# Two-block transformer kernel on one core: layers written out, attention of the first block by pairs of heads

## The chip, the cores and the metric

The kernel runs on one core of one Trainium2 chip. The metric is the device time of one execution in microseconds, as the median of several runs. The profile is of one further execution. Its engines are PE (TensorE), DVE (VectorE), ACT (ScalarE), POOL (GpSimd) and SP (SyncE, which here only issues DMAs).

## The reference, cut to what matters

256 tokens of width 1024 pass through a first block of two hybrid layers and then a second block. All arithmetic is in float32.

```
DEPTH = 2                      # layers of the first block, each with its own weights
def hybrid_layer(x, mem, ...):
    z = rms_norm(x, g_mix) @ w_in                       # 1024 x 5632
    o_a = dilated_mixer(rope(q)*s, rope(k), v)          # 2 output heads, 3 dilations each, one softmax over all
    o_b = moba_attn(rope(q)*s, rope(k), v)              # 6 heads; with 256 tokens plain causal attention
    o_m = memory_attn(q_m*s, rms_norm(mem), w_mkv)      # 4 heads over 256 memory rows
    y = gates[0]*(o_a @ w_pa) + gates[1]*(o_b @ w_pb) + gates[2]*(o_m @ w_pm)
    x = x + y @ w_o                                     # gates = sigmoid of 3 x 1024 columns of z
    return x + square(relu(rms_norm(x) @ w_up)) @ w_down   # 1024 -> 4096 -> 1024
```

The second block (`*_2` inputs) has modulation from a condition vector, latent attention with 8 heads, an mLSTM branch and 16 experts. The weights of an expert are three matrices of 1024 x 1024 (4 MB each), so 192 MB of the 393 MB that the kernel reads belong to the experts.

## The kernel before

Every layer of the first block streams its weights in 64 **units** of 1 MB (4 row chunks of 128 by 512 columns, `layer_units`). They pass through `R1 = 4` ring slots: SP issues the load of unit u when PE is done with unit u-4 (`load`, semaphore `slots_free`). Most units are **split**: ACT copies the unit in a rounded form to `ring_hi` (`split_hi`, L535), then DVE or POOL writes the rest, unit minus high part, over the unit itself, `ring_lo` (`split_lo`, L554), and PE makes three products low by high, high by low and high by high for each pair of tiles (`split_product`, L1683 to L1685). `LO_VECTOR` says which units DVE splits (4, 6, 8 and the even ones from 34), POOL does the others. The activations are held feature-major and split in the same way in `hT_hi` and `hT_lo`. Units 10 and 11 (memory keys and values) and 24 to 27 (branch projections) are plain float32 products (L1675).

A layer, in the order of PE's program: transposes of x (`half_to_features`, L1722) and units 0 to 11; rope on DVE and the transposes of q and k; **attention** with the gate units 12 to 23 in between; the branch projections, units 24 to 27, of which DVE makes y (L2051, L2060); units 28 to 31 (`w_out`), 32 to 47 (`w_up`) with the squares transposed behind each tile (`squares`, L1872), 48 to 63 (`w_down`) with small products for the modulation (L1899). The two layers are one loop body, `Fori(0, DEPTH)`, on each engine.

Attention runs in `NJ` jobs, each one head and one tile of 128 queries: 4 dilated, 12 causal, 8 memory, so 24, in 25 rounds of a pipeline. In round j, PE computes the scores of job j (L1788), transposes the weights of job j-1 (L1798), does half of a gate part (6 split products), multiplies the transposed weights of job j-1 with the values (L1821), and does the other half. DVE masks the scores and takes the maximum (L2028), ACT takes exp in SBUF with the sum (L2173), DVE divides (L2008, L2010), ACT copies the transposed weights (L2168) and the output (L2179) out of PSUM, splits a unit (L535) in every second round, and applies tanh to a finished gate (L2188).

The order on each engine is written by hand; there is no scheduler, and engines run in order. A head has 64 features, so scores use 64 of PE's 128 rows and outputs 64 of its 128 columns:

```
last = pe.matmul(flat[j % 2][:, col:col + wide * P], qkT[rows, qc, q],
                 keys[rows, kc, kt * P:(kt + wide) * P], start=True, stop=True)   # rows = 64 partitions
```

The experts run in four groups of four. PE computes the four experts of a group at once in the four 32-column strips of the array (L939), from a ring of `RE = R + 4 = 12` slots of 1 MB that SP fills in order (L612). At the end the result is scattered to tokens (L956), added to x (L1364), normalised (L1910 to L1920, L2120, L2122), multiplied with a row (L1386) and stored by one DMA (L617).

## Time and profile before

| | us |
|---|---|
| median of 3 runs (1917.25 to 1918.72) | 1918.7 |
| the profiled execution | 1913.6 |
| its span | 1911.7 |
| PE busy | 1600.2 (84%) |
| DVE busy | 606.2 (32%) |
| ACT busy | 501.0 (26%) |
| POOL busy | 487.8 (26%) |

PE is busy nine tenths or more in most slices of the first 1440 us, and seven tenths behind that, where the DMA engines are busy throughout at 421 GB/s. The busy shares say where to look; what a stretch costs is read from its length and from what its work would need without pauses.

### The profile page before, as it was taken

How to read it: one execution, taken by the hardware profiler on the slowest of the kernel's cores; microseconds unless marked ns; L12 is line 12 of the kernel's file. 1: busy time of each engine (PE TensorE's matmuls, PEld its weight loads, DVE VectorE, ACT ScalarE, POOL GpSimd, SP SyncE). 2: the span in 40 equal slices, each digit the busy share in tenths (PEclk: the TensorE clock that was granted, in tenths of full speed). 3: DMA queues.
4: the chain of work that ended last, by engine and by line, in shares of the span. 5: the costliest groups of instructions: out<-in, count | busy, mean ns of one | idle time of the engine just before them, and what ended most of it. 6: DMA issues, size and time to landing. Idle time of an engine off the chain costs nothing. (4 is left out here: it accounts for less than half of the span.)

```text
span 1911.7 us, 18589 instructions
## 1 busy us (share of the span) xinstructions
PE 1600.2 (84%) x7308; PEld 1027.1 (54%) x7308; DVE 606.2 (32%) x900; ACT 501.0 (26%) x675; POOL 487.8 (26%) x147
## 2 busy tenths in 40 slices
PE   5999989899999998989959999969768567675764
PEld 4765568777766557877657865547343113131111
DVE  4334345421524443542253126753240000000001
ACT  4254234323435433333233313423010000000000
POOL 5434162324534424433455521000000000000000
PEclk9999999999999999999979999989869889899888
DMA  6523335577543334549723462000229999999994
GB/s 217 179 92 111 110 133 176 176 285 276 166 155 98 112 124 133 176 150 351 250 66 111 133 225 93 0 13 1 77 110 399 421 422 421 421 422 421 421 422 207
DMA packets 125044, 395.49 MB, mean 207 GB/s; under 512 B 6799, under 2 KB 10692, under 8 KB 100380
## 3 DMA queue, kind: packets, MB, share of 16 engines
q1 hardware_dynamic: 123308, 389.70, 54.9%
q0 software_dynamic: 1648, 4.56, 0.7%
q8 instruction: 61, 1.00, 0.2%
q14 instruction: 27, 0.22, 0.0%
HBM read 393.18 MB, written 1.05 MB: 206 GB/s over the span
## 5 line engine op out<-in xcount | busy, mean ns | idle before, releaser
L554 POOL TENSOR_TENSOR ring_lo<-ring,ring_hi 128x2048 fp32r<-128x2048 f32 x80 | 370.0, 4629 | 546.0 <-ACT ring_hi L535 545.9
L1683 PE MATMUL psum<-ring_hi,hT_lo 128*128 128x512 f32 (+2 forms) x880 | 360.0, 409 | 36.2 <-DVE hT_lo L1927 11.7
L1685 PE MATMUL psum<-ring_hi,hT_hi 128*128 128x512 f32 (+2 forms) x880 | 347.2, 395 | 0.0
L1684 PE MATMUL psum<-ring_lo,hT_hi 128*128 128x512 f32 (+2 forms) x880 | 346.2, 393 | 0.0
L535 ACT ACTIVATE ring_hi<-ring 128x2048 fp32r<-128x2048 f32 x116 | 222.0, 1914 | 378.4 <-DMA ring<-in_w_down 138.7
L939 PE MATMUL psum<-ring,arena 128*32 128x512 f32 x1024 | 200.2, 678 | 89.4 <-DMA ring<-in_w_e_up 33.2
L1683 PEld LDWEIGHTS psum<-ring_hi,hT_lo 128*128 128x128 f32 x880 | 169.2, 192 | 80.1 <-issue 21.2
L1685 PEld LDWEIGHTS psum<-ring_hi,hT_hi 128*128 128x128 f32 x880 | 168.3, 191 | 36.6
L1684 PEld LDWEIGHTS psum<-ring_lo,hT_hi 128*128 128x128 f32 x880 | 169.0, 192 | 31.6 <-issue 0.5
L939 PEld LDWEIGHTS psum<-ring,arena 128*32 128x32 f32 x1024 | 44.0, 121 | 242.2 <-issue 83.6
L554 DVE TENSOR_TENSOR ring_lo<-ring,ring_hi 128x2048 fp32r<-128x2048 f32 x36 | 86.4, 2400 | 249.7 <-ACT ring_hi L535 249.7
L939 PE MATMUL psum<-arena 128*32 128x512 f32 x512 | 80.6, 787 | 54.3 <-DMA arena<-in_w_e_down 31.1
L1675 PE MATMUL psum<-ring,arena 128*128 128x512 f32 (+1 forms) x272 | 113.0, 574 | 0.9 <-ACT arena L2179 0.9
L547 POOL TENSOR_TENSOR ring_lo<-ring,ring_hi 128x2048 fp32r<-128x2048 f32 (+2 forms) x20 | 87.4, 4375 | 69.2 <-ACT ring_hi L542 69.2
L1683 PE MATMUL psum<-ring_hi,uT_lo 128*128 128x512 f32 x256 | 102.9, 402 | 0.0
L1684 PE MATMUL psum<-ring_lo,uT_hi 128*128 128x512 f32 x256 | 102.3, 400 | 0.0
L1685 PE MATMUL psum<-ring_hi,uT_hi 128*128 128x512 f32 x256 | 100.8, 394 | 0.0
L1675 PEld LDWEIGHTS psum<-ring,arena 128*128 128x128 f32 x272 | 51.3, 190 | 58.2 <-issue 50.6
L939 PEld LDWEIGHTS psum<-arena 128*32 128x32 f32 x512 | 19.6, 138 | 108.6 <-issue 61.3
L1545 ACT ACTIVATE arena<-psum 128x512 f32<-128x512 f32 x8 | 4.3, 595 | 248.1 <-PE psum L939 248.1
L2010 DVE TENSOR_SCALAR arena<-arena,rden 128x256 f32<-128x256 f32 (+3 forms) x48 | 60.8, 1267 | 1.7
L1683 PEld LDWEIGHTS psum<-ring_hi,uT_lo 128*128 128x128 f32 x256 | 49.2, 192 | 16.2 <-issue 5.0
(323 smaller groups left out, 1664.5 us busy)
## 6 DMA issues: line engine op xcount, KB each, us to landing
ring<-in_w_in SPq DMA_DIRECT2D x60, 1024.0 KB, 5.2
ring<-in_w_e_gate SPq DMA_DIRECT2D x48, 1024.0 KB, 20.1
ring<-in_w_e_up SPq DMA_DIRECT2D x48, 1024.0 KB, 21.6
ring<-in_w_up SPq DMA_DIRECT2D x32, 1024.0 KB, 5.2
ring<-in_w_down SPq DMA_DIRECT2D x32, 1024.0 KB, 6.1
arena<-in_w_e_down SPq DMA_DIRECT2D x32, 1024.0 KB, 19.9
ring<-in_w_e_down SPq DMA_DIRECT2D x32, 1024.0 KB, 22.3
arena<-in_w_e_gate SPq DMA_DIRECT2D x16, 1024.0 KB, 18.0
```

What stands on the lines that cost most here:

```text
L535: act.activation(slot_hi(u), slot(u), ACT.Copy).then_inc(hi_sb, 1)
L547: pool.tensor_tensor(slot_lo(u)[:, :, 0:n], slot(u)[:, :, 0:n], slot_hi(u)[:, :, 0:n].bitcast(F32), ALU.subtract)\
L554: eng.tensor_tensor(slot_lo(u), slot(u), slot_hi(u).bitcast(F32), ALU.subtract).then_inc(done, 1)
L939: mm = pe.matmul(psum[32 * j:32 * j + 32, bank + n, :], lhsT[:, 2 * q + c, 32 * j:32 * j + 32], both[:, c * D + n * UN:c * D + (n + 1) * U ...
L1545: act.activation(hid[:, n, :], psum[:, n, :], ACT.Silu).then_inc(hid_a, 1)
L1675: last = pe.matmul(dst, lhsT(k0 + k), slot(u)[:, first + k, 0:n], start=start and k == 0, stop=stop and k == nk - 1)
L1683: pe.matmul(dst, lo(k0 + k), w_hi, start=start and k == 0, stop=False)
L1684: pe.matmul(dst, hi(k0 + k), w_lo, start=False, stop=False)
L1685: last = pe.matmul(dst, hi(k0 + k), w_hi, start=False, stop=stop and k == nk - 1)
L2010: dve.tensor_scalar(S[:, i % 3, 0:wide], S[:, i % 3, 0:wide], rden[:, i:i + 1], None, ALU.mult)\
```

## The change

1. The two layers are written out (`for l in range(DEPTH)` in place of `Fori`); waits compare with constants, and the copies of per-layer data (`g_now`, `silu_now`) go. POOL splits all units except unit 0 of layer 0 and the even units from 50, which stay on DVE.
2. Attention: 13 jobs in 14 rounds. A job holds two heads of a pair, one in each half of the partitions, except the two dilated ones of the second query tile, which hold one head. PE alternates between the two heads in scores and outputs; the two heads' scores lie in different PSUM banks. ACT writes exp into PSUM over the scores, and DVE multiplies from there into SBUF for both heads in one instruction. DVE now does maximum, scale, reciprocal and multiply of job j before it turns to job j+1. The gate work is cut in 48 parts of 6 products, spread over 27 places by `gate_parts`. ACT splits one unit at the end of each of the rounds 0 to 8.
3. Branch projections: three pairs of PSUM banks in turn instead of two, and y is summed from PSUM.
4. The last squares (`squares(7)`) are transposed behind unit 48; the first half of x for the next layer is transposed in the middle of unit 63, the second half behind unit 0 of the next layer.
5. `w_out`/`w_up`: ACT makes the first half of `hT_hi` before it splits unit 34.
6. Start: x and the small rows are loaded from ACT's queue, the memory rows and large constants only when x has landed; DVE splits unit 0.
7. Experts: `RE = R + 8`, 16 slots. The last expert pass finishes one half of the columns first; the last normalisation goes tile by tile, with the table of the square root loaded ahead, and two stores.

```diff
-LO_VECTOR = [4, 6, 8] + list(range(34, UNITS1, 2))
-LO_POOL = [u for u in SPLIT if u not in LO_VECTOR]
+LO_VECTOR = [(l, u) for l in range(DEPTH) for u in SPLIT if (l == 0 and u == 0) or (u >= 50 and u % 2 == 0)]
+LO_POOL = [(l, u) for l in range(DEPTH) for u in SPLIT if (l, u) not in LO_VECTOR]
...
+    job("dilated", 0, 0, [(HD * h, dilated(h, 0)) for h in range(2)])
     for h in range(2):
+        job("dilated", 1, 0, [(HD * h, dilated(h, 1))])
+    for pair in range(3):
         for t in range(TT):
...
+            job("causal", t, 1 + pair, [(HD * i, [(6 + pair, 9 + pair, kt, ("z", 3 * WA + 2 * WB + HD * (2 * pair + i)))
+                                                  for kt in range(t + 1)]) for i in range(2)])
...
+def gate_parts(j, place):
+
+    at = lambda slot: (2 * GATE_PARTS * slot + 2 * NJ + 1) // (2 * (2 * NJ + 1))
+    slot = 2 * j + place if j < NJ else 2 * NJ
...
-RE = R + 4
+RE = R + 8
...
                         while i < len(bl):
...
+                            for h, (base, blocks) in enumerate(job["heads"]):
+                                qc, kc, kt, _ = blocks[i]
+                                rows = slice(base, base + HD)
+                                last = pe.matmul(to[:, h, i * P:(i + wide) * P], qkT[rows, qc, q],
+                                                 keys[rows, kc, kt * P:(kt + wide) * P], start=True, stop=True)
...
+                        for i in range(n):
+                            for h, (base, blocks) in enumerate(job["heads"]):
...
+                                last = pe.matmul(flat[2][base:base + HD, 768:768 + P], v, PT[:, (j - 1) % 2, h * n + i, :],
+                                                 start=i == 0, stop=i == n - 1)
...
-                        dve.tensor_scalar(S[:, i % 3, 0:wide], S[:, i % 3, 0:wide], rden[:, i:i + 1], None, ALU.mult)\
+                    dve.tensor_tensor(weights_of(j), scores(j), rden[:, c0:c0 + nh].unsqueeze(2).to_broadcast([P, nh, wide]), ALU.mult)\
...
-                    if j % 2 and 15 + j // 2 < 24:
-                        split_hi(act, l, 15 + j // 2)
...
+                    if 15 + j < 24:
+                        split_hi(act, l, 15 + j)
...
-                        part.append(z[:, :, c0:c0 + UN])
-                        dve.scalar_tensor_tensor(out=part[b], in0=part[b], scalar=1.0, in1=DB[i % 2][:, :, :],
-                                                 op0=ALU.add, op1=ALU.mult).then_inc(pj_sb, 1)
+                        part = y if b == 0 else DB[PJ[i]][:, :, :]
+                        ins = dve.scalar_tensor_tensor(out=part, in0=z[:, :, c0:c0 + UN], scalar=1.0, in1=DB[PJ[i]][:, :, :],
+                                                       op0=ALU.add, op1=ALU.mult)
...
-                squares(7)
                 for kg in range(8):
...
+                            if t == 1 and u == UNITS1 - 1 and l + 1 < DEPTH:
+                                pe.wait_ge(dn_x, 2 * l + 1)
+                                half_to_features(x, 0)
...
+                        if u == 48:
+                            squares(7)
...
-                high_parts(32, 34)
-                high_half(0, g_now[:, 2, :], l * 8 + 7)
+                high_parts(32, 33)
+                high_half(0, g_feat[:, 2, l, :], l * 8 + 7)
+                high_parts(34, 34)
```

The order that results, at three places. PE's program in the causal part of attention; L1683 to L1685 are gate products, L1788 the scores of a job, L1798 the transposes and L1821 the outputs of the job before. Before:

```order
L1821 MATMUL psum<-arena 64x128 x2
L1683 MATMUL psum<-ring_hi,hT_lo 128x512
L1684 MATMUL psum<-ring_lo,hT_hi 128x512
L1685 MATMUL psum<-ring_hi,hT_hi 128x512
L1683 MATMUL psum<-ring_hi,hT_lo 128x512
L1684 MATMUL psum<-ring_lo,hT_hi 128x512
L1685 MATMUL psum<-ring_hi,hT_hi 128x512
L1779 REGISTER_ALU
L1788 MATMUL psum<-arena 128x256
L1794 REGISTER_ALU
L1798 MATMUL psum<-consts,arena 128x128
```

The same place of the changed kernel, where L1872 are the outputs, L1848 the scores, L1727 to L1729 the gate products and L1860 the transposes; this is the first causal job behind the dilated ones:

```order
L1872 MATMUL psum<-arena 64x128 x6
L1848 MATMUL psum<-arena 128x128 x2
L1727 MATMUL psum<-ring_hi,hT_lo 128x512
L1728 MATMUL psum<-ring_lo,hT_hi 128x512
L1729 MATMUL psum<-ring_hi,hT_hi 128x512
L1727 MATMUL psum<-ring_hi,hT_lo 128x512
L1728 MATMUL psum<-ring_lo,hT_hi 128x512
L1729 MATMUL psum<-ring_hi,hT_hi 128x512
L1860 MATMUL psum<-consts,arena 128x128 x6
```

Outputs and scores now stand next to each other, both heads' matmuls in one row, and the gate products moved between scores and transposes and between transposes and outputs.

ACT in the same part of attention. Before, L2168 copies transposed weights, L2173 is exp, L2179 copies an output, L535 splits a unit:

```order
L2168 ACTIVATE arena<-psum 128x128
L2172 REGISTER_ALU
L2173 ACTIVATE arena,den<-arena,nmx 128x256
L2179 ACTIVATE arena<-psum 64x128
L535 ACTIVATE ring_hi<-ring 128x2048
L2165 REGISTER_ALU
L2168 ACTIVATE arena<-psum 128x256
L2172 REGISTER_ALU
L2173 ACTIVATE arena,den<-arena,nmx 128x128
L2179 ACTIVATE arena<-psum 64x128
```

And of the changed kernel, with exp in L2242, tanh of a gate in L2234, the copy of weights in L2251, of an output in L2257 and the split in L561:

```order
L2242 ACTIVATE psum,den<-arena,nmx 128x256 x2
L2234 ACTIVATE arena<-psum,rms 128x512
L2251 ACTIVATE arena<-psum 128x256
L2234 ACTIVATE arena<-psum,rms 128x512
L2257 ACTIVATE arena<-psum 128x128
L561 ACTIVATE ring_hi<-ring 128x2048
L2242 ACTIVATE psum,den<-arena,nmx 128x128 x2
L2251 ACTIVATE arena<-psum 128x512
```

Exp of the next job moved ahead of the copy of the weights, and the split of a unit stands at the end of every round up to round 8, where before it stood in every second.

PE at the end of `w_up`. Before, the transposes of the last two squares (L1872) follow each other ahead of the first product of `w_down` (the one with uT):

```order
L1685 MATMUL psum<-ring_hi,hT_hi 128x512
L1867 REGISTER_ALU
L1869 REGISTER_ALU
L1872 MATMUL psum<-consts,arena 128x128 x8
L1867 REGISTER_ALU
L1869 REGISTER_ALU
L1872 MATMUL psum<-consts,arena 128x128 x8
L1683 MATMUL psum<-ring_hi,uT_lo 128x512
```

In the changed kernel the one transpose group (L1919) is followed by `w_down` at once:

```order
L1728 MATMUL psum<-ring_lo,hT_hi 128x512
L1729 MATMUL psum<-ring_hi,hT_hi 128x512
L1919 MATMUL psum<-consts,arena 128x128 x8
L1727 MATMUL psum<-ring_hi,uT_lo 128x512
L1728 MATMUL psum<-ring_lo,uT_hi 128x512
L1729 MATMUL psum<-ring_hi,uT_hi 128x512
```

The other group of eight moved behind the 24 products of unit 48.

## Rows read from the trace of the kernel before

**Rows 1.** Busy time of each engine by stretch (us), PE clock, DMA share, GB/s

```profile
24.60:102.50 77.90, 77.05 (x320) 58.16 (x320) 37.18 (x44) 26.76 (x26) 39.92 (x10) 1.00 0.49 160
102.50:223.30 120.80, 112.98 (x509) 75.43 (x509) 48.71 (x120) 54.70 (x118) 42.42 (x10) 1.00 0.30 97
223.30:304.50 81.20, 72.88 (x279) 51.42 (x280) 33.99 (x30) 27.10 (x29) 37.29 (x8) 0.96 0.44 144
304.50:376.30 71.80, 71.80 (x338) 59.13 (x337) 35.80 (x30) 28.58 (x19) 27.94 (x7) 1.00 0.54 176
376.30:384.20 7.90, 1.90 (x11) 1.67 (x10) 5.97 (x5) 2.17 (x2) 0.00 (x0) 0.82 0.40 133
...
485.50:491.20 5.70, 2.02 (x18) 1.75 (x17) 2.88 (x5) 2.68 (x9) 1.07 (x1) 1.00 0.57 190
...
566.70:687.50 120.80, 112.96 (x509) 75.46 (x509) 48.71 (x120) 54.71 (x118) 41.85 (x10) 1.00 0.30 97
...
1430.00:1887.50 457.50, 309.79 (x1657) 93.53 (x1658) 20.26 (x29) 14.00 (x25) 0.00 (x0) 0.89 0.99 413
```

**Rows 2.** PE's groups by shape in attention, 102.5 to 223.2 us

```profile
L1683 PE MATMUL psum<-ring_hi,hT_lo 128*128 128x512 f32 x96 | 42.3, 440 | 4.7 <-ACT arena L2188 4.7
...
L1821 PE MATMUL psum<-arena 128*64 128x128 f32 x104 | 16.5, 284 | 1.4 <-ACT arena L2168 1.4
L1788 PE MATMUL psum<-arena 64*128 64x256 f32 x40 | 12.9, 418 | 0.0
L1798 PE MATMUL psum<-consts,arena 128*128 128x128 f32 x52 | 10.9, 297 | 1.2 <-DVE arena L2010 1.2
L1788 PE MATMUL psum<-arena 64*128 64x128 f32 x24 | 4.8, 306 | 0.9 <-ACT arena L2160 0.9
```

**Rows 3.** Pieces of the chain that ended last: start, us, what

```profile
1857.86 3.73 PE psum L939 x32
...
1895.50 3.71 PE psum L956 x8
```

**Rows 4.** Timelines of DVE and POOL in attention and in the branch projections

```profile
133.09 0.35 DVE L2010 TENSOR_SCALAR arena<-arena,rden 128x256 f32<-128x256 f32 x1
...
136.85 3.38 DVE L2010 TENSOR_SCALAR arena<-arena,rden 128x128 f32<-128x128 f32 x1
...
249.18 4.63 DVE L2060 TENSOR_TENSOR xn<-xn,arena 128x1024 f32<-128x1024 f32 x1
...
135.58 4.57 POOL L554 TENSOR_TENSOR ring_lo<-ring,ring_hi 128x2048 fp32r<-128x2048 f32 x1 [6.23 <-ACT ring_hi L535]
...
248.15 14.67 POOL L554 TENSOR_TENSOR ring_lo<-ring,ring_hi 128x2048 fp32r<-128x2048 f32 x3 [1.31 <-ACT ring_hi L535]
```

**Rows 5.** Who waited for whom: 223.3 to 305 us, then 376 to 385 us

```profile
PE psum L1683 <- DVE hT_lo L1927: 4.9, 1, 4.9
...
PE psum L1722 <- DVE xn L2060: 3.4, 1, 3.4
...
PE psum L1872 <- DVE arena L2098: 6.0, 1, 6.0
```

**Rows 6.** PE's timeline at the start, SP's at the experts, DVE's and ACT's at the end

```profile
24.61 0.80 PE L1683 MATMUL psum<-ring_hi,hT_lo 128*128 128x512 f32 x1 [6.47 <-POOL ring_lo L554]
...
1434.94 2.07 SPq L612 DMA_DIRECT2D ring<-in_w_e_gate  x4
...
1901.66 1.28 ACT L2122 ACT_TABLE_LOAD   x1
...
1903.40 1.42 DVE L1920 TENSOR_SCALAR xn<-x,stat 128x1024 f32<-128x1024 f32 x2
...
1904.92 2.36 DVE L1386 TENSOR_TENSOR xn<-xn,arena 128x1024 f32<-128x1024 f32 x2
```

**Rows 7.** DMA issue with its landing time, and ACT's group of unit splits

```profile
ring<-in_w_in SPq DMA_DIRECT2D x60, 1024.0 KB, 5.2
...
L535 ACT ACTIVATE ring_hi<-ring 128x2048 fp32r<-128x2048 f32 x116 | 222.0, 1914 | 378.4 <-DMA ring<-in_w_down 138.7 <-DMA ring<-in_w_up 109.2 <-DMA ring<-in_w_in 71.8
```

More of the change, by code:

```diff
@@ L123 @@
 NJ = len(JOBS)
+NH = sum(len(job["heads"]) for job in JOBS)
+GATE_PARTS = 8 * 6
+def gate_parts(j, place):
+    at = lambda slot: (2 * GATE_PARTS * slot + 2 * NJ + 1) // (2 * (2 * NJ + 1))
+    slot = 2 * j + place if j < NJ else 2 * NJ
+    if j == NJ and place == 0:
+        return range(0)
+    return range(at(slot), at(slot + 1))
 def z_column(chunk):
@@ L272, in build @@
         turn_lo = sem("turn_lo")
-        gains = sem("gains")
         mem_g = sem("mem_g")
@@ L406, in build @@
         row_in = sem("row_in")
-        quad_in = sem("quad_in")
-        ctx_in = sem("ctx_in")
+        quad_in = [sem(f"quad_in{i}") for i in range((RE - R) // 4)]
         x_row = sem("x_row")
@@ L931, in experts @@
                 for q in rounds:
-                    for c in range(2):
-                        for n in range(2):
+                    ends = g == NE // EG - 1 and part == 2 and q == 3
+                    for c, n in ((0, 0), (1, 0), (0, 1), (1, 1)) if ends else ((0, 0), (0, 1), (1, 0), (1, 1)):
                             for j in range(EG):
@@ L943, in experts @@
                                     mm.then_inc(slots_free, 1)
+                            if ends and c == 1 and n == 0:
+                                mm.then_inc(y_half, 1)
             def gather(g):
@@ L1774, in _, with gate_part @@
                 pe.wait_ge(km_sb, l + 1)
+                def gate_part(p):
+                    g, kh, t, half = p // 8, p // 4 % 2, p // 2 % 2, p % 2
+                    u = 12 + p // 4
+                    if p % 4 == 0:
+                        unit_ready(u, l)
+                    if g and kh == 0 and half == 0:
+                        pe.wait_ge(g_tanh, l * 12 + 2 * (g - 1) + t + 1)
+                    last = split_product(DB[3][:, t, :], tokens(hT_hi, t), tokens(hT_lo, t), UC * kh + 2 * half, u, nk=2,
+                                         first=2 * half, start=kh == 0 and half == 0, stop=kh == 1 and half == 1)
+                    if kh == 1 and half == 1 and t == 0:
+                        last.then_inc(g_full, 1)
+                    if half == 1 and t == 1:
+                        last.then_inc(slots_free, 1)
@@ L1784, in _ @@
+                        i, bl = 0, job["heads"][0][1]
                         while i < len(bl):
-                            qc, kc, kt, _ = bl[i]
-                            wide = 2 if i + 1 < len(bl) and bl[i + 1][1] == kc else 1
-                            keys = kmT if job["kind"] == "memory" else qkT
-                            last = pe.matmul(flat[j % 2][:, col:col + wide * P], qkT[rows, qc, q],
-                                             keys[rows, kc, kt * P:(kt + wide) * P], start=True, stop=True)
@@ L2102, in _ @@
                 low_squares(7)
-                for u in range(52, UNITS1, 2):
+                for u in range(50, UNITS1, 2):
                     split_lo(dve, l, u)
```

475 lines of the change are left out of this document (244 added, 231 removed).

## The prediction

> **What bounds the kernel now.** I read the stretches first. In the first block PE is the engine that ends every stretch: `w_up` is 71.8 us of PE busy in 71.8, the first stretch 77.05 in 77.9, and the two layers are alike to 0.1 us (the two lines of 120.80) [rows 1]. In the experts it is the stream of weights: DMA share 0.99 at 413 GB/s while PE is busy 310 of 457 us [rows 1]. So a gain must be PE's in the first block, or bytes taken out of the stream behind 1430 us, or work behind the last byte. Everything in front of the stream shifts it by as much, since its first reload is issued when PE has consumed the first expert units, at 1434.94 [rows 6].
>
> A busy PE is not yet a PE at its best, so I count work. `w_up` is a yardstick: 288 split products and 48 transposes in 71.8 us without idle time [rows 1]. A full float32 pass of 512 columns costs 3.71 / 8 = 0.46 us [rows 3].
>
> **Attention, 120.8 us a layer.** It has the same 288 split products (96 in each of three lines) and 52 transposes: 71.8. Scores: 40 instructions of 256 and 24 of 128 columns, 13,312 columns or 26 passes of 512, 12.0 us. Outputs: 104 of 128 columns, 26 passes, 12.0 us [rows 2]. Sum 95.8. Of the other 25.0 us, 8.2 are idle time in front of PE (4.7 + 1.4 + 1.2 + 0.9) [rows 2], and 16.8 lie between instructions, 0.70 for each of 24 jobs; I put these down to the changes between gate products, scores and outputs, four in a job.
>
> After: two jobs with one head keep 12 score and 24 output instructions, 2.8 + 2.8 us. The other 18.4 us come in pairs that use different halves of the array. What a pair gains in scores (row halves) no row shows. The nearest row is the experts': 32 instructions in four column strips take 3.73 us where 8 full ones take 3.71, so four strips run together nearly free [rows 3]. Bounds for a pair are a factor of 1 and of 2. I take 1.6, since outputs have 128 columns each against the experts' 512, with the same weight load in front: 18.4 becomes 11.5. Work is 71.8 + 5.6 + 11.5 = 88.9. Changes: 13 jobs by 0.70 = 9.1. Idle: the waits for DVE's multiply go, since a pair's multiply reads PSUM; the tail stays, about 1.5. A new one comes: ACT splits unit 15+j at the end of round j, whose load may be issued only when unit 11+j is consumed, and from round 2 on that is the same round. The load takes 5.2 us, the split 1.9 [rows 7], a round about 7; what is queued behind it on ACT is exp of the next job and the copy of the weights, for which PE's outputs wait. PE has between them some 6 us of gate products, so I charge 2 us a layer (bounds 0 and 8). Total 101.5, 19.3 less; **38.6 for two layers**. Bounds: all of it ideal 94, nothing gained by pairs and ACT late 112.
>
> The change of DVE's operands is weighed here. The same multiply takes 0.35 us for 256 columns from SBUF, and 3.38 us for 128 columns when it starts inside a split of POOL that lasts until 140.15 [rows 4]. Two heads cost at best 0.70, so one instruction of 512 columns from PSUM may take as long without a loss. The Trainium skill, "VectorE: DVE Perf Modes", section "Why PSUM operands drop a tier", speaks against the change: float32 from PSUM has only the single rate. By it the multiply would be twice as long per column; with 7 us a round and under 4 us of DVE work in it, the sum stays the same by either.
>
> **Branch projections and `w_out`, 81.2 us a layer.** Work: 8 split units with 32 transposes are two thirds of the yardstick, 47.9, and 48 float32 passes 22.3: 70.2. Missing are 3.4 us of waiting for DVE's y, 4.9 for the low part of the first half [rows 5], and 2.7 us in which the clock was 0.96 of full speed on average [rows 1]. The first wait is the sum of y in SBUF, 4.63 us for 1024 columns inside POOL's run of three splits [rows 4]; from PSUM it should take about 1.2 and be done before unit 28 ends. Then POOL's unit 29 is next, ready some 4 us early. The second is ACT: it splits unit 34 first, whose load waits for unit 30, and only then makes the half of `hT_hi` that PE needs. The new order takes this away; unit 34 comes 1.6 us later and is needed 12 us later. I take 10 of 11.0, **20 for both layers** (bounds 12 and 22).
>
> **The last squares.** PE waits 6.0 us for DVE [rows 5] in a stretch of 7.9, in which the transposes are 0.9. Behind unit 48 (24 products, 5.6 us) the squares are there. **14 for both** (12 to 16).
>
> **POOL** takes the units that DVE had: one of 4.6 us [rows 4] for each 24 products, 5.6 us of PE by the yardstick (with its transposes 6.0). It keeps up by 1 us a unit. From the release of a slot to its use PE has three units, 17 us; load 5.2, split 1.9 and low part 4.6 are 11.7. Charged at nothing; what hides it is that slack.
>
> **Start.** PE's first product waits for POOL's low part until 24.61 [rows 6]. Ring loads leave SP earlier, behind four small ones and not behind x and eight row loads, and DVE halves the 4.6 us of the first low part. I take 4.5 of what I bound by 2 and 7, less than half a microsecond of it lost to the transposes now inside.
>
> **Layer boundary,** 5.7 us [rows 1]: the transposes of x move inside, but ACT now splits unit 2 ahead of the first half of `hT_hi`, and its load waits for unit 62: done(62) + 5.2 + 1.9 + 2 for the half. That is about 3 us behind unit 63, and 1.9 of transposes are still paid. 0.5.
>
> **Experts.** 180 loads of 1 MB go through behind 1434.94 until 1887.5, 2.51 us each [rows 1, 6]. Four more are in place beforehand: they are released with `w_out` of the second block and have its routing to land in. **10.0.**
>
> **End.** Table load 1.28, both tiles' scaling 1.42 and one of two final multiplies 1.2 [rows 6] leave the chain, and half of the eviction in front of the scatter, with the last column half under the PE work, 1.2. **5.1.**
>
> Sum: 38.6 + 20 + 14 + 4.5 + 0.5 + 10 + 5.1 = 92.7. Against the profiled execution, 1913.6, that is 1820.9. The median of the runs shown is 5.1 higher, so 1826 on its scale. Writing out the layers by itself I charge at nothing: registers for waits are set in the sequencers while engines are busy.
>
> **Rivals.**
> (a) Pairs do not overlap. For: no row shows row halves running together. Against: the experts' strips [rows 3]. Then 18.4 stays 18.4: 6.9 a layer, 1840.
> (b) Only outputs fail to overlap. Scores load 128 weight columns into different rows, outputs load both heads' weights into the same rows. For: with 128 columns the load is as long as the product; experts have 512. Factor 1 on 9.2 us in place of 1.6 costs 3.5 a layer, 1833. The Trainium skill, "TensorE: Matmul & The Clock Gate", section "Part 3: Packing small matmuls", has a rule of this kind: a weight load overlaps running products only if its row group differs.
> (c) Attention becomes a chain, PE waiting for exp and copies in each round. For: DVE now stays with one job from maximum to multiply and ACT carries a split in each round. Against: some 7.5 us of gate products lie between scores and transposes of a job, and maximum, exp and multiply of two heads are about 4.5. It gives nothing back when a round takes 120.8 / 13.5 = 9 us: 1865.
> (d) POOL becomes the bound and the kernel slower. Its run of three splits beside DVE took 14.67, 4.9 each [rows 4]. PE would wait for each of 101 low parts beyond 5.6 us. To eat 92.7 us a split must take 6.5; at 7.0 the time is 1965.
> (e) Everything overlaps, ACT never waits and the start gives 7: 1808.
>
> **How the numbers follow.** Forecast 0.50, (a) 0.10, (b) 0.15, (c) 0.10, (d) 0.02, (e) 0.13. The likeliest's own range is 1812 to 1842. The range of 1796 to 1856 takes in (a), (b) and (e) and the bounds of the projections, and leaves out (c), (d) and the far ends. Faster by over 0.2% (about what a measurement of this kernel tells from no change): 0.97; within it 0.01; slower 0.02.
>
> **What would show it.** Attention from the first score to the first projection product 97 to 106 us in both layers; the score and output groups' spacing halved; no multiply of DVE above 1 us; ACT waiting for ring loads in rounds 4 to 8, and PE for ACT by a microsecond or two behind it. `w_up` to `w_down` without a pause; projections and `w_out` 71 us at a clock of 1.00; stream start to last landing 443 us. Wrong if PE shows waits for POOL's low parts of over 1 us each, if a score pair takes as long as two single ones, or if the second block, which I leave as it is, moves.

## The result, and the profile after

The changed kernel takes 1808.3 us in the median of 4 runs (1802.45 to 1810.55); the kernel before took 1918.0 beside it. The ratio is 0.9426 [0.9402, 0.945], so it is faster. The forecast was 1826, its range 1796 to 1856, so the time lies inside and 18 us under the middle. Of these 18, 12.9 are the prediction's terms; the other 5 are the 5.1 that it added to get from the profiled execution to the median, and in the changed kernel the two are alike (1807.95 and 1808.3). The profiled execution took 1807.95 us, its span is 1806.2, the PE clock 0.928.

The stretches of the first block and the stream, the same view as [rows 1]. As in the prediction, the stretch called branch projections and `w_out` reaches to the first product of unit 36, so it holds the first four units of `w_up` (32 to 35), and the 71.8 us called `w_up` are units 36 to 47. (The columns: busy time of PE, PEld, DVE, ACT, POOL; clock; DMA share; GB/s.)

```profile
19.40:98.10 78.70, 77.83 (x330) 58.87 (x330) 17.74 (x37) 31.77 (x34) 52.05 (x12) 1.00 0.53 171
98.10:197.50 99.40, 95.36 (x508) 71.50 (x508) 25.36 (x87) 48.64 (x96) 41.77 (x10) 0.98 0.35 113
197.50:266.90 69.40, 69.40 (x279) 49.23 (x280) 25.63 (x29) 26.78 (x29) 45.01 (x10) 1.00 0.54 174
266.90:338.70 71.80, 71.80 (x338) 59.10 (x337) 23.04 (x25) 29.03 (x19) 56.48 (x13) 1.00 0.55 176
338.70:440.10 101.40, 101.34 (x499) 76.29 (x497) 26.71 (x16) 32.92 (x19) 43.03 (x9) 1.00 0.83 290
440.10:443.30 3.20, 0.02 (x1) 0.03 (x1) 1.74 (x5) 2.16 (x5) 2.42 (x1) 1.00 0.65 177
443.30:521.30 78.00, 77.12 (x329) 58.31 (x329) 18.80 (x38) 30.06 (x33) 47.46 (x11) 0.98 0.53 167
521.30:620.60 99.30, 95.35 (x508) 71.55 (x508) 25.48 (x87) 48.69 (x96) 41.81 (x10) 0.98 0.35 112
...
1346.70:1789.30 442.60, 299.97 (x1627) 91.46 (x1616) 20.45 (x32) 14.43 (x26) 0.00 (x0) 0.82 1.01 417
```

Attention goes from 120.8 to 99.4 us, the branch projections and `w_out` from 81.2 to 69.4, both in both layers [rows 1]. The separate stretch of the last squares is gone, and what follows it is not longer for the squares that moved in: 101.4 us with them. The stream is 10 us shorter. The pause between the layers is 3.2 us instead of 5.7, but the stretch behind it is 78.0 instead of 75.5: the moved transposes are inside, and its clock is 0.98 instead of 1.00. Beside the prediction's terms, measured between the same instructions in both traces:

| term | predicted | measured |
|---|---|---|
| attention, two layers | 38.6 | 42.6 |
| projections and `w_out`, two layers | 20 | 23.6 |
| last squares | 14 | 15.5 |
| start (first score of layer 0) | 4.5 | 4.5 |
| layer boundary | 0.5 | 0.0 |
| expert stream | 10.0 | 10.0 |
| end, behind the last landing | 5.1 | 7.3 |
| rest (`w_down` of layer 1 1.1, second block 1.0) | 0 | 2.1 |
| sum (the spans, 1911.7 and 1806.2, differ by 105.5) | 92.7 | 105.6 |

### The profile page after: what moved, and what is told of

The parts are those of the page before. It is cut to its first block and busy times, and to the rows that moved or that the text cites. A ratio compares the mean times of both kernels' runs of the same rounds, so it can differ in the third digit from the quotient of the medians.

```text
span 1806.2 us, 17176 instructions
## 1 busy us (share of the span) xinstructions
PE 1544.8 (86%) x7308; PEld 1009.5 (56%) x7308; DVE 490.7 (27%) x810; ACT 492.4 (27%) x641; POOL 581.1 (32%) x158
## 3 DMA queue, kind: packets, MB, share of 16 engines
HBM read 393.18 MB, written 1.05 MB: 218 GB/s over the span
## 5 line engine op out<-in xcount | busy, mean ns | idle before, releaser
L580 POOL TENSOR_TENSOR ring_lo<-ring,ring_hi 128x2048 fp32r<-128x2048 f32 x101 | 467.8, 4636 | 374.0 <-ACT ring_hi L561 374.0
L1727 PE MATMUL psum<-ring_hi,hT_lo 128*128 128x512 f32 (+2 forms) x880 | 355.8, 404 | 22.0 <-DVE hT_lo L1978 10.7
L1729 PE MATMUL psum<-ring_hi,hT_hi 128*128 128x512 f32 (+2 forms) x880 | 345.7, 393 | 0.0
L561 ACT ACTIVATE ring_hi<-ring 128x2048 fp32r<-128x2048 f32 x116 | 222.0, 1915 | 392.2 <-DMA ring<-in_w_in 123.0
L966 PE MATMUL psum<-arena 128*32 128x512 f32 x768 | 132.4, 854 | 94.7 <-DMA arena<-in_w_e_down 35.6
L1727 PEld LDWEIGHTS psum<-ring_hi,hT_lo 128*128 128x128 f32 x880 | 167.6, 190 | 64.1 <-DVE hT_lo L1978 12.1
L1729 PEld LDWEIGHTS psum<-ring_hi,hT_hi 128*128 128x128 f32 x880 | 167.5, 190 | 37.2
L966 PE MATMUL psum<-ring,arena 128*32 128x512 f32 x768 | 138.8, 701 | 43.5 <-DMA ring<-in_w_e_gate 18.3
L966 PEld LDWEIGHTS psum<-arena 128*32 128x32 f32 x768 | 30.6, 148 | 196.6 <-issue 80.2
L966 PEld LDWEIGHTS psum<-ring,arena 128*32 128x32 f32 x768 | 32.2, 124 | 142.6 <-issue 59.2
L1727 PE MATMUL psum<-ring_hi,uT_lo 128*128 128x512 f32 x256 | 101.9, 398 | 0.0
L1729 PE MATMUL psum<-ring_hi,uT_hi 128*128 128x512 f32 x256 | 100.4, 392 | 0.0
L1728 PE MATMUL psum<-ring_lo,uT_hi 128*128 128x512 f32 x256 | 99.4, 388 | 0.0
L580 DVE TENSOR_TENSOR ring_lo<-ring,ring_hi 128x2048 fp32r<-128x2048 f32 x15 | 42.1, 2806 | 101.7 <-ACT ring_hi L561 101.7
L568 ACT ACTIVATE ring_hi<-ring 128x2048 fp32r<-128x2048 f32 (+2 forms) x20 | 35.8, 1806 | 84.2 <-DMA ring<-in_w_in 84.2
L1727 PEld LDWEIGHTS psum<-ring_hi,uT_lo 128*128 128x128 f32 x256 | 48.1, 188 | 14.3 <-issue 5.0
```

What stands on the lines that cost most here:

```text
L561: act.activation(slot_hi(u), slot(u), ACT.Copy).then_inc(hi_sb, 1)
L568: act.activation(slot_hi(u)[:, :, 0:n], slot(u)[:, :, 0:n], ACT.Copy).then_inc(hi_sb, 1)
L580: eng.tensor_tensor(slot_lo(u), slot(u), slot_hi(u).bitcast(F32), ALU.subtract).then_inc(done, 1)
L966: mm = pe.matmul(psum[32 * j:32 * j + 32, bank + n, :], lhsT[:, 2 * q + c, 32 * j:32 * j + 32], both[:, c * D + n * UN:c * D + (n + 1) * U ...
L1727: pe.matmul(dst, lo(k0 + k), w_hi, start=start and k == 0, stop=False)
L1728: pe.matmul(dst, hi(k0 + k), w_lo, start=False, stop=False)
```

## Inside attention

PE's groups in attention of layer 0, the same view as [rows 2]:

```profile
L1727 PE MATMUL psum<-ring_hi,hT_lo 128*128 128x512 f32 x96 | 40.8, 425 | 1.3 <-ACT arena L2234 1.3
...
L1872 PE MATMUL psum<-arena 128*64 128x128 f32 x104 | 9.8, 284 | 1.9 <-ACT arena L2251 1.9
L1848 PE MATMUL psum<-arena 64*128 64x256 f32 x40 | 8.6, 446 | 0.0
L1860 PE MATMUL psum<-consts,arena 128*128 128x128 f32 x52 | 7.8, 273 | 0.5 <-ACT arena L2257 0.5
L1848 PE MATMUL psum<-arena 64*128 64x128 f32 x24 | 2.4, 304 | 0.9 <-ACT arena L2222 0.9
```

The counts are those of [rows 2], and the mean of one output is still 284 ns, but their busy time together fell from 16.5 to 9.8, and that of the large scores from 12.9 to 8.6. When the mean stays and the sum of time falls, the instructions overlap more than before. (Each float32 `pe.matmul` of scores or outputs is two rows of the trace; the counts here are rows.) Pieces of two rounds in PE's timeline (start, length):

```profile
139.87 0.65 PE L1874 MATMUL psum<-arena 128*64 128x128 f32 x4
140.45 0.48 PE L1850 MATMUL psum<-arena 64*128 64x128 f32 x2
...
144.31 0.69 PE L1850 MATMUL psum<-arena 64*128 64x256 f32 x2
```

This is the run below with one head in a job (L1874 outputs, L1850 scores): 4 outputs take 0.58 us from start to start, 2 scores of 256 columns are 0.69 long. The changed kernel, with both heads:

```profile
140.36 0.66 PE L1872 MATMUL psum<-arena 128*64 128x128 f32 x8
140.94 0.70 PE L1848 MATMUL psum<-arena 64*128 64x256 f32 x4
```

8 outputs take 0.58, 4 scores are 0.70 long. The factor of a pair is 2.0 in scores and in outputs, where I had taken 1.6 between bounds of 1 and 2.

The new wait that I charged with 2 us is there too. ACT's unit splits and, behind them, PE:

```profile
143.87 1.92 ACT L561 ACTIVATE ring_hi<-ring 128x2048 fp32r<-128x2048 f32 x1 [2.53 <-DMA ring<-in_w_in]
...
160.11 1.92 ACT L561 ACTIVATE ring_hi<-ring 128x2048 fp32r<-128x2048 f32 x1 [4.37 <-DMA ring<-in_w_in]
```

```profile
ACT ring_hi L561 <- DMA ring<-in_w_in: 12.6, 5, 4.4
```

```profile
PE psum L1872 <- ACT arena L2251: 1.9, 1, 1.9
PE psum L1727 <- ACT arena L2234: 1.3, 1, 1.3
```

The first two rows are ACT's timeline, the others the waits (us in total, times, longest). ACT stands 12.6 us in front of loads, the copy of the weights (L2251) is queued behind that, and PE waits 1.9 us for it. The windows before and behind this gap show what follows:

```profile
155.98:163.80 7.82, 6.03 (x28) 4.60 (x26) 2.74 (x7) 3.69 (x8) 3.83 (x2) 1.00 0.47 142
164.27:169.29 5.02, 5.02 (x19) 3.59 (x17) 1.08 (x5) 2.47 (x4) 2.44 (x2) 0.67 0.45 175
```

Behind the pause PE is busy throughout at a mean granted clock of 0.67 of full speed, so for a part of these 5 us it ran at the lower of its levels, 1.2 instead of 2.4 GHz. 12 products take 4.0 us there and 3.0 in the round before. The four scores right behind the gap, of 256 columns, take 1.23 us for the 0.70 of the same group above. A pause of 1.9 us cost over 3 in all.

## The experiments

Times between sessions are compared through the kernel before, whose median lay between 1914.1 and 1918.0; stretches are compared in the traces, where code that did not change repeats within 0.2 us as long as PE does not pause. Where it does, the clock moves: the attention of the changed kernel, with the same program, took 97.7 to 99.5 us in the five runs that contain it, and the second block varied by 7 us. So effects of 1 us in attention, or of 5 in the whole kernel, are not read from one run.

| run | time, us | ratio | attention, two layers |
|---|---|---|---|
| changed kernel | 1808.3 | 0.9426 [0.9402, 0.945] | 99.4, 99.3 |
| single heads | 1832.2 | 0.9568 [0.9552, 0.9584] | 109.5, 109.5 |
| heads apart | 1811.2 | 0.9457 [0.9441, 0.9473] | 98.6, 98.4 |
| later split | 1801.7 | 0.9419 [0.9403, 0.9435] | 94.3, 94.3 |
| ring of 12 | 1818.4 | 0.9508 [0.9492, 0.9524] | 99.0, 99.4 |
| squares in front | 1817.5, one run | | 99.5, 97.8 |
| unit 34 first | 1822.6, one run | | 97.7, 99.2 |
| before, written out | 1914.2 | 0.9996 [0.9982, 1.0009] | 120.7, 120.9 |
| splits on DVE | 1803.4, one run | | 97.9, 97.8 |
| later split, boundary | 1795.7 | 0.9374 [0.9361, 0.9387] | 94.3, 94.3 |
| same columns | 1812.9, one run | | 99.2, 99.1 |
| y in SBUF | 1814.5, one run | | 94.3, 94.3 |
| multiply in SBUF | 1803.4, one run | | 94.3, 94.3 |

### One head in a job

```diff
-            job("causal", t, 1 + pair, [(HD * i, [...]) for i in range(2)])
+            for i in range(2):
+                job("causal", t, 1 + pair, [(HD * i, [...])])
...
-                    if 15 + j < 24:
-                        split_hi(act, l, 15 + j)
+                    if j % 2 and 15 + j // 2 < 24:
+                        split_hi(act, l, 15 + j // 2)
```

> The changed kernel (1808.3 us, attention 99.4 us a layer) with one head in each job again: 24 jobs in 25 rounds, ACT splitting a unit in every second round, everything else as changed. Theory, the pairs did it: the two heads of a pair run at the same time on PE, so 18.4 us of scores and outputs a layer become 9.2 in the changed kernel; taking the pairs away gives those 9.2 back, and 11 more jobs at 0.70 us of changes are 7.7, less about 2.5 of ACT's late splits, which go. Attention 111 to 115 us a layer, the kernel 1832 to 1840. Rival, the jobs' number does not matter and the gain came from DVE's order, the multiply out of PSUM and the evenly spread gate parts: attention at most 103 us, the kernel at most 1816. Between them, about 106: only the overlap or only the changes count.

109.5 us in both layers: 10.1 more than with pairs, 11.2 less than before. It lies between the two, so neither theory holds alone. Between the starts of PE's instructions, waits taken out, scores are 16.0 us against 10.0 and outputs 15.0 against 9.1 in pairs, 11.8 together, and the rest of the groups 0.7 more. From that go 2.5 us of waits that the pairs bring. Of the 11.2 us that have nothing to do with pairs, 6.2 are waits: 7.7 us in front of PE before, 1.5 now. (The 0.9 in front of the first score lie ahead of the stretch in both and are not counted; the 0.4 and 0.5 in front of the first projection product at its end are.) Those of before stand in [rows 2]; these are the ones of this run up to that product (us in total, times, longest):

```profile
PE psum L1850 <- ACT arena L2224: 0.9, 1, 0.9
PE psum L1874 <- ACT arena L2253: 0.6, 1, 0.6
PE psum L1862 <- ACT arena L2259: 0.5, 1, 0.5
```

The 4.7 us of waits for tanh (L2188 before) are gone; a gate's tile is now released for tanh by itself and the parts are spread; I did not try these two apart. The other 5.0 us are denser groups, of which 2.7 in the transposes; which of the new orders gives them stays open.

### The heads not in turn

```diff
-                        for i in range(n):
-                            for h, (base, blocks) in enumerate(job["heads"]):
+                        for h, (base, blocks) in enumerate(job["heads"]):
+                            for i in range(n):
```

and the same in the scores.

> The changed kernel with the jobs left in pairs, but in scores and in outputs PE does all matmuls of the first head and then all of the second, instead of one of each in turn. It tells overlap from fewer changes. Theory A, the two heads overlap on PE only when their matmuls stand next to each other: about three quarters of the pairs' 9.2 us a layer are lost (the last matmul of one head and the first of the other still meet), attention 99.4 to about 106 us, the kernel 1820 to 1824. Theory B, the changed kernel's gain in attention is from 13 jobs for 24 and from the waits that went, and the matmuls of the two heads follow one another anyway: no change, attention within 1 us of 99.4.

Theory A falls. Groups with two or four matmuls a head take the same time in either order: 0.63 us for 4 scores, 0.59 for 8 outputs. Only the longest feel it. The scores of the first job, six for each head, behind a wait:

```profile
97.05 1.23 PE L1848 MATMUL psum<-arena 64*128 64x128 f32 x12 [0.87 <-ACT arena L2222]
```

```profile
98.06 0.94 PE L1848 MATMUL psum<-arena 64*128 64x128 f32 x12 [0.88 <-ACT arena L2222]
```

The first row is this run, 1.23 us, the second the changed kernel, 0.94. Theory B's number holds, no change, but not its reason: if the matmuls of the two heads followed one another, 8 outputs would take twice the 0.58 us of 4, and not 0.59. So PE overlaps the second head with the first though four matmuls of the first stand in between, and for part of a group of six. Writing them in turn is worth 0.3 us in a long group and nothing in a short one. That attention is 0.9 us shorter than in the changed kernel is within what the clock does.

### ACT splits one round later

```diff
-                    if 15 + j < 24:
-                        split_hi(act, l, 15 + j)
+                    if 1 <= j < 10:
+                        split_hi(act, l, 14 + j)
```

> The changed kernel, but ACT splits unit 14+j at the end of round j (rounds 1 to 9) instead of unit 15+j (rounds 0 to 8), so that the load has landed when ACT comes to it. In the changed kernel ACT waits 12.6 us for loads in attention, and PE shows gaps of 1.9, 1.3 and 0.5 us behind ACT with a lower clock after the longest. Theory, ACT's early split is what costs: these gaps and the slow products behind them go, attention 99.4 to 96 or 97 us a layer, the kernel 1802 to 1805. Rival, PE now waits for POOL's low part, which starts a round later: attention the same or longer, with PE waiting for ring_lo in the gate products.

94.3 us in both layers, 5.1 less where I expected 2 to 3. PE's waits in attention, complete:

```profile
PE psum L1848 <- ACT arena L2222: 0.9, 1, 0.9
PE psum L1860 <- ACT arena L2257: 0.5, 1, 0.5
```

ACT waits for no load any more, and the two gaps are gone, 3.2 us. The other 1.9 are the slow products: the clock of the stretch is 1.00 for 0.98. POOL's low parts are in time. By the whole time this run can't be told from the changed kernel (0.9419 against 0.9426), since the second block varies by more; the trace can.

### The ring of 12 slots

```diff
-RE = R + 8
+RE = R + 4
```

> The changed kernel with a ring of 12 slots for the experts, as before, in place of 16. Theory, four loads fewer behind the moment at which PE releases the first expert slot: 4 by 2.51 = 10.0 us more, the kernel 1818, stream from start to last landing 452.5 us. Rival, the stream's length is the same because its start only moved: no change within 2 us.

1818.4 us, and from the first reload, issued at 1346.7 us as in the changed kernel, to the last landing 452.5 us:

```profile
1799.37 4.05 PE L966 MATMUL psum<-arena 128*32 128x512 f32 x20 [4.72 <-DMA arena<-in_w_e_down]
```

The changed kernel has that row at 1789.31: 10.1 us for four loads of 2.51.

### The last squares in front again

```diff
-                        if u == 48:
-                            squares(7)
...
+                squares(7)
                 for kg in range(8):
```

> The changed kernel with the last squares transposed in front of unit 48 again instead of behind it. Theory, only the place of that group counts: PE waits some 6 us for DVE there, as before, in both layers; the stretch from unit 32 to the first product of w_down 71.8 to about 79 us (before 79.7 and 79.4), w_down 0.5 to 1 us shorter, the kernel 13 to 14 us longer. Rival, with POOL splitting the even units DVE is free earlier and the wait was mostly DVE's own splits: the stretch is at most 76 us, the kernel at most 8 us longer.

The rival is right. The stretch is 75.1 and 74.8 us, 3.1 more than 71.8 and not 7; 1.9 of the 3.1 are a wait, the rest mostly the transposes that are back inside. PE's wait is a third of the 6.0 of [rows 5]:

```profile
PE psum L1919 <- DVE arena L2143: 1.9, 1, 1.9
```

The other 4.1 us before had been DVE's own. It stood in a split that waited for ACT, and only then took the tile, whose last product PE had ended at 375.71, 4.1 us earlier:

```profile
375.32 0.39 PE L1685 MATMUL psum<-ring_hi,hT_hi 128*128 128x512 f32 x1
377.59 2.29 DVE L554 TENSOR_TENSOR ring_lo<-ring,ring_hi 128x2048 fp32r<-128x2048 f32 x1 [6.27 <-ACT ring_hi L535]
379.80 1.22 DVE L2095 TENSOR_SCALAR arena<-psum 128x1024 f32<-128x1024 f32 x1
```

Those are rows of before; here DVE takes the tile at 337.81, as soon as PE is done, with nothing ahead of it. The whole time of this one run is 9.2 us above the changed kernel's, more than the rival's 8; by the trace 4.0 of them are there when the second block begins, and the rest is that block, which varies by more.

### Unit 34 split first again

```diff
-                high_parts(32, 33)
+                high_parts(32, 34)
                 high_half(0, g_feat[:, 2, l, :], l * 8 + 7)
-                high_parts(34, 34)
```

> The changed kernel with ACT splitting unit 34 again in front of the first half of the high part of x, between w_out and w_up. Projections and w_out were 81.2 us a layer before and 69.4 with the change. Theory, ACT's order was the 4.9 us wait: that stretch goes to 73.5 to 74.5 us a layer, the kernel 8 to 10 us longer. Rival, that wait came mostly of DVE, which split unit 34 itself before the low part and now does not: at most 2 us a layer.

The stretch of projections and `w_out` is 74.8 us in layer 0 and 75.0 in layer 1, 5.5 more than the 69.4, a little over what the theory gave: a wait of 3.7 us and a clock of 0.98. The whole time is 14.2 us more in this one run; 9.2 of them are there when the second block begins, within the 8 to 10 of the theory.

```profile
PE psum L1727 <- DVE hT_lo L1978: 3.7, 1, 3.7
```

### Before, with the layers written out

```diff
-            with pe.Fori(0, DEPTH) as l:
+            for l in range(DEPTH):
```

on each of the five engines.

> The kernel before with nothing changed but the layer loop written out on each of the five engines; the per-layer copies, the splitting of units among engines and every order stay. Theory, writing out gives nothing by itself: within 1 us of before in each stretch, the time within 0.2%. Rival, the register arithmetic in front of the waits costs where PE issues short groups: attention shorter by 2 to 5 us a layer, since its transposes took 6.5 us there for 52 against 3.8 in the changed kernel with single heads, and the time 0.2 to 0.5% shorter.

Ratio 0.9996 [0.9982, 1.0009], attention 120.7 and 120.9 us. Registers cost nothing, and the denser transposes are not theirs.

### DVE splits its units again

```diff
-LO_VECTOR = [... if (l == 0 and u == 0) or (u >= 50 and u % 2 == 0)]
+LO_VECTOR = [... if (l == 0 and u == 0) or u in (4, 6, 8) or (u >= 34 and u % 2 == 0)]
```

and the calls on DVE as before, that of unit 34 behind the low part.

> The changed kernel with the units 4, 6, 8 and the even ones from 34 split on DVE again. Theory, POOL has the slack and nobody waits for it: no stretch changes by more than 1 us except where DVE is slowed, the kernel within 3 us. Rival, the two engines get in each other's way when both work in SBUF: each split takes longer on both, and PE waits for DVE's eviction of w_up tiles, 2 to 8 us longer.

1803.4 us in one run, 4.9 less than the changed kernel where the theory allowed 3, which one run does not tell from nothing; no stretch of the first block is longer than in the changed kernel by more than 0.4 us, `w_up` 71.7 us. With the last squares behind unit 48 it does not matter who splits: the squares' new place and the splits' new engine each cover the same wait, and together they don't add.

### The boundary, and the best version

```diff
-                    high_parts(2, 2)
                     high_half(0, g_feat[:, 0, l, :], l * 8 + 1)
+                    high_parts(2, 2)
```

with the later split.

> The best version so far (ACT's split of a gate unit one round later), and between the layers ACT makes the first half of the high part of x before it splits unit 2 of the next layer. In the run with the later split PE's first product of layer 1 came at 437.34 us, 3.28 us late behind DVE's low part; ACT had the half's transposes by about 432 and first waited until 432.96 for the load of unit 2 and then split it for 1.9. Theory, ACT's order is that wait: the pause between the layers goes from 3.7 to under 1.5 us, the stretches otherwise as in that run (attention 94.3 us in both layers), the kernel 2 to 3 us shorter than it. Rival, unit 2's low part is then late, and PE waits behind POOL within unit 2 for as much. Against the changed kernel as a whole the theory expects 8 to 13 us, 0.5 to 0.7%.

PE has no pause between the layers. From its last product of `w_down` to the first of layer 1 are 0.3 us for 3.6, and the stretch behind it is 1.5 shorter at a clock of 1.00:

```profile
433.50:510.00 76.50, 75.62 (x331) 57.22 (x330) 18.97 (x38) 30.88 (x34) 50.08 (x12) 1.00 0.55 179
```

Up to attention of layer 1 that is 4.9 us less than in the changed kernel, and twice 5.1 in attention come to it. The time is 1795.7, ratio 0.9374 [0.9361, 0.9387], whose interval lies below that of the changed kernel: 0.5% faster than it. Against the run with the later split alone the median is 6.0 us shorter, where I expected 2 to 3, and in the traces the way from the first product of `w_down` to attention of layer 1 is 6.0 us shorter too; I had counted the pause and not the clock behind it. It is the fastest version here. Some 5 of the 15 us of the stretches don't show in the whole; in the profile they are lost in the second block, whose code is the same.

### Both heads' outputs in the same columns

```diff
+                                if len(job["heads"]) == 2:
+                                    to = flat[2][0:HD, 768 + h * P:768 + (h + 1) * P]
```

with the heads one after the other and a second copy on ACT.

> The version with the later split, but in the outputs both heads of a pair use the same 64 columns of the array (head 2 into other PSUM columns of the same 64 partitions, copied out by a second small ACT instruction), one head after the other; scores as before. It tells where the overlap of outputs comes from. Theory, the two column halves of the array work at the same time: without them a group of 8 outputs takes not 0.59 but about 1.1 us, a group of 4 about 0.65 for 0.37; outputs 9.1 to 14 or 15 us a layer, attention 94.3 to 99 or 100. Rival, the array plays no part and the weight loads of 64 columns simply hide behind the product before: the groups stay at 0.59 and attention within 1.5 us of 94.3.

```profile
135.25 0.65 PE L1875 MATMUL psum<-arena 128*64 128x128 f32 x4
135.84 0.49 PE L1848 MATMUL psum<-arena 64*128 64x128 f32 x4
...
141.07 1.09 PE L1875 MATMUL psum<-arena 128*64 128x128 f32 x8
142.09 0.70 PE L1848 MATMUL psum<-arena 64*128 64x256 f32 x4
```

Four outputs take 0.59 us for 0.37, eight take 1.02 for 0.59, attention 99.2 us for 94.3. The theory holds: it is the two column halves that run together. For the scores no such run was made, but the rates exclude the rival there too: by [rows 3] a full pass of 512 columns takes 3.71 / 8 = 0.46 us, so four scores of 256 columns, two passes, would take 0.93 us one after the other even with every weight load hidden, and they take 0.63 from start to start. By the Trainium skill, "TensorE: Matmul & The Clock Gate", "Part 3: Packing small matmuls", a weight load overlaps running products only if its row group differs; both heads' loads go to all rows here, and the pairs still reach a factor of 2.0, so in this case the rule, if read as a bar to the overlap, does not hold.

### y summed in SBUF

```diff
-                        part = y if b == 0 else DB[PJ[i]][:, :, :]
+                        part = y if b == 0 else z[:, :, c0:c0 + UN]
```

with the later split.

> The version with the later split, but two of the three gated branches go back into SBUF, where y is summed from SBUF operands alone, as before. Theory, an addition on DVE with both operands in SBUF cannot start or finish while POOL splits units: it takes not 1.2 but 3 to 5 us when it falls on one, and PE waits for y in front of its transposes by about 3.4 us; the stretch from the first product of w_out to unit 32 48.25 to 51 or 52 us. Rival, the wait was from the order of DVE's steps and the two PSUM buffers, and goes with three buffers: the stretch within 1 us of 48.25.

Two additions of DVE, and POOL in the same stretch:

```profile
211.50 5.53 DVE L2106 TENSOR_TENSOR xn<-xn,arena 128x1024 f32<-128x1024 f32 x1
...
219.32 3.63 DVE L2106 TENSOR_TENSOR xn<-xn,arena 128x1024 f32<-128x1024 f32 x1
```

```profile
206.94 9.01 POOL L580 TENSOR_TENSOR ring_lo<-ring,ring_hi 128x2048 fp32r<-128x2048 f32 x2 [31.62 <-ACT ring_hi L561]
217.28 10.13 POOL L580 TENSOR_TENSOR ring_lo<-ring,ring_hi 128x2048 fp32r<-128x2048 f32 x2 [1.34 <-ACT ring_hi L561]
```

From PSUM all of these take 1.22 us. PE waits 3.7 us, though in front of `w_out` and not of the transposes, and the stretch is 75.0 us for 69.4. So the theory's cause holds, additions that last as long as POOL's splits, but neither its place nor its size: the stretch that it named, from the first product of `w_out` to unit 36 (48.25 us; the expectation says unit 32), is 49.6 and not 51 or 52, because the wait lies ahead of it, and the whole costs 5.6 us a layer, 3.7 of wait and the rest the clock behind it.

### The multiply in SBUF

```diff
-                            act.activation(scores(j)[:, h, :], weights_of(j)[:, h, :], ACT.Exp, ...
+                            act.activation(weights_of(j)[:, h, :], weights_of(j)[:, h, :], ACT.Exp, ...
...
-                    dve.tensor_tensor(weights_of(j), scores(j), rden...
+                    dve.tensor_tensor(weights_of(j), weights_of(j), rden...
```

with the later split.

> The version with the later split, but ACT writes exp back into SBUF and DVE multiplies there, for both heads in one instruction, as the kernel before did with one head. Theory, out of PSUM the multiply is free of POOL: in SBUF, within one of POOL's 4.6 us splits, it takes 3 to 5 us instead of 0.7, in most rounds; PE then waits for it in front of the transposes in some rounds, attention 94.3 to 97 or more. Rival, with 3.5 us of gate products between scores and transposes and one multiply a round the delay is covered: attention within 1 us of 94.3 although the multiply is slow.

DVE's multiplies, and POOL's split beside the first of them:

```profile
131.27 4.02 DVE L2077 TENSOR_TENSOR arena<-arena,rden 128x512 f32<-128x512 f32 x1
...
184.03 0.69 DVE L2077 TENSOR_TENSOR arena<-arena,rden 128x512 f32<-128x512 f32 x1
```

```profile
130.13 4.61 POOL L580 TENSOR_TENSOR ring_lo<-ring,ring_hi 128x2048 fp32r<-128x2048 f32 x1 [2.41 <-ACT ring_hi L561]
```

The multiply that starts inside a split ends at 135.29, 0.55 us behind POOL's end at 134.74; without POOL it takes 0.69, the same as from PSUM. The others do the same: those of 256 columns end 0.28 us behind POOL's split (0.42 alone), the one of 768 columns 0.82 (0.96 alone). So it does not run slowly, it stands until POOL is done. The Trainium skill, "SBUF — State Buffer", "SBUF: two separate sides", says this of DVE instructions with two SBUF inputs beside a POOL instruction that reads SBUF: whoever comes first holds the shared ports for its whole instruction. The trace agrees. And yet attention is 94.3 us, as from PSUM. Nine multiplies of about 4 us cost PE nothing, because a round leaves them room. The rival is right.

## Why the prediction was right, point by point

**Attention.** The terms were right, and one was mis-sized: the pair factor, taken as 1.6 of bounds 1 and 2, measures 2.0. The 18.4 us then become 9.2 and not 11.5, 2.3 a layer, 4.6 in all; that is more than the 4.0 by which attention beat its 38.6. In the row that I took it from, the experts' four strips, the overlap was nearly free, and I marked it down for the shorter columns without a row. The 0.70 us for each of 24 jobs, called changes between groups, came out in sum (8.4 us, for 7.7) but not as explained. Without waits, the step from 24 jobs to 13 gave 12.6 us; less the 9.2 of overlap that is 3.4 for 11 jobs, 0.3 each, and the other 5.0 had come with the new order while the jobs were still 24. The 12.6 are net of the 1.9 us that the lower clock took: with the later split, at a clock of 1.00, the step is 14.6, and 12.6 of it lie in scores and outputs alone. The groups that pair up took 25.1 us one head at a time, from start to start, and not the 18.4 of their passes, and they halve whole, with what stands around the passes; so most of what I had called changes belongs to the overlap. Waits fell by 3.7, for 4.7. The wait of ACT for loads is where it was said to be; charged 2 us, it is 3.2 of gaps and up to 1.9 of lower clock. Rivals (a) and (b) are out by the measured factor, (b) also by the run with the same columns. (c) is out: DVE and ACT keep up with 7 us a round even with multiplies of 4. From PSUM the multiply takes 0.42, 0.69 and 0.96 us for 256, 512 and 768 columns, 1.05 ns for each further column; before, out of SBUF and with POOL idle, 0.35 us for 256 and 0.62 for 768, 0.52 ns. So it is twice as long per column, as the prediction allowed for, and no multiply is above 1 us.

**Projections and `w_out`.** 11.8 us a layer for 10. ACT's order is worth 5.5 (said: 4.9 of wait), y from PSUM 5.6 (said: 3.4 of wait); each includes the clock behind its pause, which I had as a term of its own of 2.7.

**Last squares.** The sum was right, 15.5 for 14, its reason only in part: with the splits on POOL, 3.1 a layer of the stretch hung on the place. Either edit hides most of the wait, which two runs show.

**POOL** charged at nothing: right, 101 splits of 4.6 us and no wait of PE for one; (d) is out, and having the splits on DVE changes nothing either. (The 1965 that (d) names is not its own sum: 101 splits of 7.0 against 5.6 us are 141 us on 1826, 1967.)

**Start** 4.5, **boundary** 0 for 0.5 and **experts** 10.0 were right. The experts have a run of their own, the boundary one for ACT's order alone; the start and the end have none, so there only the sums are compared. At the boundary what the transposes took out came back in the next stretch, 1.0 us as transposes and 1.5 as lower clock (78.0 us at 0.98 against 76.5 at 1.00 with ACT's order turned), and the pause that remained was ACT's order, as costed. **End** 7.3 for 5.1: the last PE pass took 5.13 us for 6.71 before, at a granted clock of 0.70 for 0.56. That is luck and no work of the change: in the fastest version the same code took 6.6 us at 0.54. Without it the end is 5.7.

Of (e), that everything overlaps, the first half happened; ACT waited all the same. That the time of 1808 is its number is luck: it comes from 4.0 us more than forecast in attention, 3.6 in the projections, 1.5 in the squares, 2.2 at the end and 2.1 that no term named, less 0.5 at the boundary, and from the 5.1 between profile and median that the changed kernel did not show. The 94 that the prediction gave as the ideal attention is what the later split reached, 94.3.

## What to carry to other kernels

Ask of a stall not only its length but what the clock does behind it, and which other edit of the same change already covers it: here pauses of 3 to 4 us cost half as much again, and two edits covered one wait. Put an in-order engine's work that waits for a DMA behind what another engine needs next; three such orders on ACT were worth 5.1 us a layer in attention, 5.5 a layer ahead of `w_up` and 4.9 between the layers, without a line of new work. Two heads of 64 belong side by side in the array for twice the rate, in either order up to four rows a head and in turn at six; an instruction with two SBUF inputs on DVE beside long POOL instructions is worth moving only if somebody waits for it.

## What the runs showed of the hardware that was not expected

Matmuls of 64 rows or 64 columns overlap with those of the other half though four of their own half stand between them (8 outputs 0.59 us in either order); at six and six part of it is lost (1.23 us for 0.94). A DVE instruction with two SBUF operands that fell into a POOL instruction ended as if it had begun when that was over: 0.28, 0.55 and 0.82 us behind POOL's end, where alone it takes 0.42, 0.69 and 0.96. So 0.69 us of work took 4.02. Behind a PE pause of 1.9 us the granted clock was 0.67 of full speed over 5.0 us of unbroken work, and 12 products took 4.0 us for 3.0. At the start the same ACT order as at the boundary is left (PE's first product at 19.38 us, behind a split that waited for its load); that wasn't tried.
